# Where six weight buffers and one activation buffer start in SBUF: a layout change in a float32 decoder trunk

## The chip, the cores and the metric

The kernel runs on one core of a Trainium2 chip. The metric is device time in microseconds (us). Engines are named as the profile names them: PE is TensorE (its weight loads are PEld), DVE is VectorE, ACT is ScalarE, POOL is GpSimd, SP is SyncE, which issues most DMAs.

## What is computed

Two decoder layers over 256 tokens of width 1024, all in float32. Layer 0 is a gated linear recurrence with an input projection to 4096 columns and an output projection, then a dense SwiGLU of inner width 2816. Layer 1 is sliding-window attention with a shared key/value projection, then a mixture of 8 experts of inner width 3584, two experts per token.

```python
h = h + hgrn2_mixer(rmsnorm(h), w_in, lb, g_norm, w_out)      # 1024 -> 4096, 1024 -> 1024
h = h + (silu(hn @ w_gate) * (hn @ w_up)) @ w_down             # 1024 -> 2816 -> 1024
k, v = rmsnorm(h) @ kv_w                                       # 1024 -> 512
h = h + swa_attention(rmsnorm(h), k, v, w_q, w_o)              # 1024 -> 1024, twice
h = h + moe_swiglu(rmsnorm(h), router, w_gate, w_up, w_down)   # 8 experts, top 2
```

## The kernel before

The dense stages (everything up to the experts) stream their weights in 63 chunks of 128 partitions x 2048 columns (8 KB a partition). A chunk c lands by DMA in `raw[:, c % 6]`. A product in float32 is made of three matmuls in the reduced format fp32r: ACT copies the chunk, rounded, to `w_hi[:, c % 3]` (line 626), DVE subtracts to get the remainder in `w_lo[:, c % 3]` (line 916), and the activations are split the same way, into `ht_hi` and `ht_lo` for most stages, `mid_hi` and `mid_lo` for the SwiGLU's inner values, `kv_hi` and `kv_lo` for keys and values. `product` (lines 1442 to 1444) then issues hi x hi, hi x lo, lo x hi. Each matmul has two operands in SBUF: the stationary one, 128 columns that a weight load brings into the array, and the moving one, 256 or 512 columns that stream through. The weight load of the next matmul runs beside the moving stream of the present one.

In `to_features` the weights are stationary and the activations move: chunks 0 to 7 and the SwiGLU's 22 gate and up chunks (20 to 41). In `to_rows` the activations are stationary and the weights move: chunks 8 to 15, the outputs 16 to 19 (512 columns wide), the SwiGLU's down chunks 42 to 52 (512 wide), keys 53 and values 58 (256 wide, with `kv_hi`/`kv_lo`), queries 54 to 57 and attention output 59 to 62 (512 wide). In both, the streams that run beside each other come in one order: moving hi beside the load of hi, moving lo beside the load of lo, moving hi beside the load of the next hi.

The expert stage is a loop over expert blocks (8 in this run), each with 46 loads; its matmuls are plain float32 of 32 stationary columns, four of them abreast in the array's column strips, and take their moving operands from a ring made of `raw` and `more_ring` (lines 1888 and 1900). `more_ring` begins where `w_hi` began.

Buffers are laid one behind another, each start rounded up to 32 bytes. In bytes of a partition, `raw` begins at 16512, `h` at 65664, `ht_hi` at 73856, `ht_lo` at 82048, `w_hi` at 114880, `w_lo` at 139456, `mid_hi` at 164032, `mid_lo` at 186560, `kv_hi` at 207040, `kv_lo` at 215232. Modulo 512 bytes that is 128 for `raw`, `h`, `ht_hi` and `ht_lo`, and 192 for all the others. Slots of `w_hi`, `w_lo` and `raw` are 8192 bytes apart, the 128-column pieces that a matmul takes are multiples of 512 bytes apart, so every piece has its buffer's remainder.

Of the kernel before, what the change touches and what calls it, by code (L numbers as in the profile page):

```python
# [9 lines left out]
P = 128  # L10
# [19 lines left out]
CW = 2048  # L30
RAW, SPLIT = 6, 3
# [66 lines left out]
def build_program(nc, a, out):  # L98
    f32, f32r = mybir.dt.float32, mybir.dt.float32r
    i32, u32 = mybir.dt.int32, mybir.dt.uint32  # L100
    ALU, ACT, AX = mybir.AluOpType, mybir.ActivationFunctionType, mybir.AxisListType
    MUL, ADD, SUB = ALU.mult, ALU.add, ALU.subtract

    def plain(ap):
        return ap.bitcast(f32)
# [36 lines left out]
    ctx = ExitStack()  # L142
    with ctx:
        def sb(stack, name, shape, dt=f32):
            return stack.enter_context(nc.sbuf_tensor(name, shape, dt))

        def sem(name):
            return ctx.enter_context(nc.semaphore(name))


        raw = sb(ctx, "raw", [P, RAW, CW])
        h = sb(ctx, "h", [P, TT, D])
        with ExitStack() as over:

            early = sb(over, "early", [P, TT, 2, D])
        ht_hi = sb(ctx, "ht_hi", [P, KT, T], f32r)
        ht_lo = sb(ctx, "ht_lo", [P, KT, T], f32r)
        xs = sb(ctx, "xs", [P, TT, D])
        const = sb(ctx, "const", [P, K_END])
# [24 lines left out]
        early_slot = sb(ctx, "early_slot", [P, TT, 2], u32)  # L184

        dense = ExitStack()
        w_hi = sb(dense, "w_hi", [P, SPLIT, CW], f32r)
        w_lo = sb(dense, "w_lo", [P, SPLIT, CW], f32r)
        s = ExitStack()
        fT = sb(s, "fT", [P, HEADS, T])  # L190
        qT = sb(s, "qT", [P, HEADS, T])
# [49 lines left out]
        slot = sb(ctx, "slot", [P, TT, 2, 4], u32)  # L241
# [39 lines left out]
        hi_ready = sem("hi_ready")  # L281
        split_ready = sem("split_ready")
# [35 lines left out]
        first_hi = sem("first_hi")  # L318
        first_lo = sem("first_lo")
# [73 lines left out]
            return banks[c % 4] if c < 12 else banks[4 + c % 2]  # L393

        def split_view(buf, c, width):
            return buf[:, c % SPLIT, :].rearrange("p (k c) -> p k c", c=width)


        def ring_place(k):
# [211 lines left out]
        def _(act):  # L611
# [9 lines left out]
            def round_chunk(c, slot_raw, raw_count, slot):  # L621
                act.wait_ge(raw_full[slot_raw], raw_count)

                if not (isinstance(c, int) and c < SPLIT):
                    act.wait_ge(chunk_used, c - (SPLIT - 1))
                nc.scalar.activation(w_hi[:, slot, :], raw[:, slot_raw, :], ACT.Copy).then_inc(hi_ready, 1)  # L626

            def round_to(c_last):

                while nxt[0] <= c_last:  # L630
                    c = nxt[0]
                    round_chunk(c, c % RAW, 16 * (c // RAW + 1), c % SPLIT)
                    nxt[0] += 1
# [44 lines left out]
            def round_x(pairs):  # L678
                for u in pairs:
                    act.wait_ge(fresh_turned, u + 1)  # L680
                    for k in range(2):
                        kt = 2 * u + k
                        ins = nc.scalar.activation(ht_hi[:, kt, :], FRESH_1[u][:, T * k:T * k + T], ACT.Copy,
                                                   scale=cols[:, kt:kt + 1])
                    ins.then_inc(fresh_hi, 1)

            half_chunk = lambda buf, part: buf[:, 0, 1024 * part:1024 * part + 1024]
            act.wait_ge(turn_free, 1)
            round_x((0, 1))
            act.wait_ge(first_full, 16)  # L690
            nc.scalar.activation(half_chunk(w_hi, 0), half_chunk(raw, 0), ACT.Copy).then_inc(first_hi, 1)
            round_x((2, 3))
            act.wait_ge(raw_full[0], 16)
            nc.scalar.activation(half_chunk(w_hi, 1), half_chunk(raw, 1), ACT.Copy).then_inc(hi_ready, 1)
            nxt[0] = 1
            round_to(LEAD - 1)
            act.wait_ge(x_loaded[1], 16)
# [7 lines left out]
            for c in range(N_IN):  # L705
# [10 lines left out]
                part, i = divmod(c, 4)  # L716
# [186 lines left out]
        def _(dve):  # L903
# [9 lines left out]
            def rest_chunk(c, slot_raw, slot):  # L913

                dve.wait_ge(hi_ready, c + 1)
                nc.vector.tensor_tensor(w_lo[:, slot, :], raw[:, slot_raw, :], plain(w_hi[:, slot, :]), SUB).then_inc(split_ready, 1)  # L916

            def rest_to(c_last):
                while nxt[0] <= c_last:
                    c = nxt[0]  # L920
                    rest_chunk(c, c % RAW, c % SPLIT)
                    nxt[0] += 1
# [54 lines left out]
            def rest_x(pairs):  # L977
                for u in pairs:
                    dve.wait_ge(fresh_hi, u + 1)
                    for k in range(2):  # L980
                        kt = 2 * u + k
                        ins = nc.vector.scalar_tensor_tensor(
                            out=ht_lo[:, kt, :], in0=FRESH_1[u][:, T * k:T * k + T], scalar=cols[:, kt:kt + 1],
                            in1=plain(ht_hi[:, kt, :]), op0=MUL, op1=SUB)
                    ins.then_inc(fresh_lo, 1)

            half_chunk = lambda buf, part: buf[:, 0, 1024 * part:1024 * part + 1024]
            rest_x((0, 1))
            dve.wait_ge(first_hi, 1)
            nc.vector.tensor_tensor(half_chunk(w_lo, 0), half_chunk(raw, 0), plain(half_chunk(w_hi, 0)), SUB).then_inc(first_lo, 1)  # L990
            rest_x((2, 3))
            dve.wait_ge(hi_ready, 1)
            nc.vector.tensor_tensor(half_chunk(w_lo, 1), half_chunk(raw, 1), plain(half_chunk(w_hi, 1)), SUB).then_inc(split_ready, 1)
            nxt[0] = 1
            rest_to(LEAD - 1)
            turn_copy(cols[:, 16:64], 48)
# [35 lines left out]
            for c in range(N_IN):  # L1032
# [38 lines left out]
                if c == 7:  # L1071
# [6 lines left out]
                    k = 0  # L1078
# [17 lines left out]
                if c in (11, 12, 13):  # L1096
                    j = c - 11
                    k = sum(NCH - 1 - jj for jj in range(j))
# [330 lines left out]
            for t in range(TT):  # L1429
                for half in range(2):  # L1430
                    part = h[:, t, 512 * half:512 * half + 512]
# [4 lines left out]
        def _(pe):  # L1436
# [50 lines left out]
            def to_features(c, bank, hi, lo, fresh=None):  # L1487

                pe.wait_ge(split_ready, c + 1)
                wh, wl = split_view(w_hi, c, 256), split_view(w_lo, c, 256)  # L1490
                for half in range(2):
                    for k in range(KT):
                        if half == 0 and fresh is not None and k in fresh:
                            pe.wait_ge(fresh_lo, fresh[k])
                        cut = slice(P * half, P * half + P)
                        ins = product(bank[:, 256 * half:256 * half + 256], (wh[:, k, cut], wl[:, k, cut]),
                                      (hi[:, k, :], lo[:, k, :]), k == 0, k == KT - 1)
                ins.then_inc(chunk_used, 1)

            def to_rows(c, width, kts, k0, n_k, hi, lo, dst, since=None, tell=False, fresh=None, then_turn=None):  # L1500


                pe.wait_ge(split_ready, c + 1)
                wh, wl = split_view(w_hi, c, width), split_view(w_lo, c, width)
                for t in range(TT):
                    for q in range(max(1, width // 512)):
                        w = min(width, 512)
                        for k in range(kts):
                            kt = k0 + k
                            if t == q == 0:  # L1510
                                split_since(since, kt)
                            if fresh is not None and q == 0 and (t, k) in fresh:
                                pe.wait_ge(fresh_lo, fresh[t, k])
                            tok = slice(P * t, P * t + P)
                            cut = slice(w * q, w * q + w)
                            ins = product(dst(t, q), (hi[:, kt, tok], lo[:, kt, tok]), (wh[:, k, cut], wl[:, k, cut]),
                                          kt == 0, kt == n_k - 1)
                        if k0 + kts == n_k and tell == "parts" and (t, q) != (1, 1):
                            ins.then_inc(part_done, 1)
                        if then_turn is not None and (t, q) == (1, 0):  # L1520
                            turn_fresh(0, 0, then_turn)
                            turn_fresh(0, 1, then_turn)
                    if t == 0 and tell == "tile" and k0 + kts == n_k:
                        ins.then_inc(tile_done, 1)
                ins.then_inc(chunk_used, 1)
                if then_turn is not None:
                    turn_fresh(1, 0, then_turn)
                    turn_fresh(1, 1, then_turn)
# [434 lines left out]
```

## Time and profile before

| | |
|---|---|
| median of 3 runs | 1325.21 us |
| the runs | 1325.21, 1326.4, 1322.11 us |
| span of the profiled execution | 1321.3 us |
| of it, up to the expert loop | 444.1 us |
| of it, the expert loop | 869 us |
| PE busy | 1299.1 us (98%) |
| DVE busy, ACT busy | 360.1 us (27%), 246.4 us (19%) |

The profiled execution's span is 3.9 us (0.3%) under the median of the runs; a run's time may hold a little more than the span from first to last instruction. A matmul's recorded duration (276 ns for 256 columns) is longer than the distance between two matmuls' starts, since they are pipelined. What a matmul costs is that distance, its cadence, and it is read from the start times.

### The profile page before, as it was taken

The numbers are of one execution on the slowest core, as the hardware profiler recorded it, in microseconds if no ns is written. First come the engines' busy times: TensorE is split into PE (matmuls) and PEld (weight loads), VectorE is DVE, ScalarE is ACT, GpSimd is POOL, SyncE is SP. The second block draws the span as 40 slices with busy tenths as digits, with TensorE's granted clock in tenths as the row PEclk, the third lists the DMA queues.
The fourth block names the chain that finished last, engine by engine and source line by source line (L and its number), as shares of the span: only waits on it lengthen the run. The fifth ranks groups of instructions, "written<-read, shape, count | busy, mean of one in ns | idle before, by whom it ended". The sixth has DMA issues, their size and how long they took to land.

```text
span 1321.3 us, 32549 instructions
## 1 busy us (share of the span) xinstructions
PE 1299.1 (98%) x14662; PEld 879.8 (67%) x14662; DVE 360.1 (27%) x539; ACT 246.4 (19%) x370; POOL 56.0 (4%) x50
## 2 busy tenths in 40 slices
PE   8999999999899999999999999999999999999998
PEld 8998899988767533555745655665574575566565
DVE  5875555554875401000000100100100010010011
ACT  5554544443743100000000000000000000000000
POOL 1001000000000320000000000000000000001600
PEclk9999999999999899999999999999999999999999
DMA  9866555565522899999999999999999999999992
GB/s 321 269 210 225 185 182 177 187 223 191 184 96 72 360 421 420 415 419 418 416 419 419 418 418 418 418 410 419 419 404 420 418 407 418 416 409 414 419 413 110
DMA packets 114199, 442.52 MB, mean 335 GB/s; under 512 B 9284, under 2 KB 55700, under 8 KB 83348
## 3 DMA queue, kind: packets, MB, share of 16 engines
q1 hardware_dynamic: 107904, 424.75, 81.5%
q10 hardware_dynamic: 4820, 11.53, 2.5%
q0 software_dynamic: 1344, 4.20, 0.8%
q8 instruction: 120, 1.97, 0.6%
q14 instruction: 11, 0.09, 0.0%
HBM read 434.12 MB, written 12.08 MB: 338 GB/s over the span
## 4 chain that ended last, share of the span: by engine, by line
PE 93%; DVE 3%; ACT 2%; issue 1%; DMA 0%; ACTq 0%; DVEq 0%
PE bank L1888 44%; PE bank L1900 22%; PE bank L1442 8%; PE bank L1444 8%; PE bank L1443 8%; PE bank L1689 1%; PE bank L1600 1%; DVE w_lo L916 1%; ACT w_hi L626 0%; PE bank L1865 0%; DMA const<-in_shape_constants 0%; ACT ht_hi L654 0%; PE bank L1744 0%; PE bank L1940 0%; DVE q_from L1100 0%
## 5 line engine op out<-in xcount | busy, mean ns | idle before, releaser
L1888 PE MATMUL bank<-more_ring,xT 128*32 128x512 f32 (+1 forms) x3456 | 341.0, 545 | 0.0
L1888 PEld LDWEIGHTS bank<-more_ring,xT 128*32 128x32 f32 x3456 | 164.2, 110 | 163.5 <-issue 84.4
L1888 PE MATMUL bank<-raw,xT 128*32 128x384 f32 (+1 forms) x2688 | 259.3, 532 | 0.7 <-DVE xT L1352 0.7
L1888 PEld LDWEIGHTS bank<-raw,xT 128*32 128x32 f32 x2688 | 122.4, 110 | 127.0 <-issue 76.6
L1411 DVE TENSOR_TENSOR e_hid<-e_silu,bank 128x384 f32<-128x384 f32 (+1 forms) x48 | 26.9, 616 | 542.3 <-PE bank L1888 542.3
L1900 PE MATMUL bank<-more_ring,hidT 128*32 128x256 f32 x3072 | 171.4, 379 | 0.0
L916 DVE TENSOR_TENSOR w_lo<-raw,w_hi 128x2048 fp32r<-128x2048 f32 x62 | 141.5, 2289 | 99.1 <-ACT w_hi L626 99.0
L1900 PEld LDWEIGHTS bank<-more_ring,hidT 128*32 128x32 f32 x3072 | 120.8, 110 | 46.4
L1442 PE MATMUL bank<-ht_hi,w_hi 128*128 128x256 f32 x464 | 129.4, 279 | 1.5 <-DVE ht_lo L930 1.5
L1900 PE MATMUL bank<-raw,hidT 128*32 128x256 f32 x2304 | 129.9, 379 | 0.0
L1444 PE MATMUL bank<-ht_hi,w_lo 128*128 128x256 f32 x464 | 128.9, 278 | 0.0
L1443 PE MATMUL bank<-ht_lo,w_hi 128*128 128x256 f32 x464 | 128.9, 278 | 0.0
L626 ACT ACTIVATE w_hi<-raw 128x2048 fp32r<-128x2048 f32 x62 | 118.6, 1918 | 38.7 <-PE bank L1444 38.3
L1900 PEld LDWEIGHTS bank<-raw,hidT 128*32 128x32 f32 x2304 | 91.0, 110 | 37.9 <-issue 0.6
L889 ACT ACTIVATE e_silu<-bank 128x384 f32<-128x384 f32 (+1 forms) x48 | 22.6, 544 | 392.8 <-PE bank L1888 392.8
L1442 PEld LDWEIGHTS bank<-ht_hi,w_hi 128*128 128x128 f32 x464 | 87.9, 189 | 2.5 <-issue 2.4
L1443 PEld LDWEIGHTS bank<-ht_lo,w_hi 128*128 128x128 f32 x464 | 87.9, 189 | 0.0
L1444 PEld LDWEIGHTS bank<-ht_hi,w_lo 128*128 128x128 f32 x464 | 87.9, 189 | 0.0
L892 ACT ACTIVATE yb<-bank 96x512 f32<-96x512 f32 x8 | 4.7, 593 | 441.6 <-PE bank L1900 441.6
L1442 PE MATMUL bank<-w_hi,ht_hi 128*128 128x256 f32 (+1 forms) x224 | 74.4, 332 | 3.7 <-DVE ht_lo L944 1.6
L1444 PE MATMUL bank<-w_hi,ht_lo 128*128 128x256 f32 (+1 forms) x224 | 73.2, 327 | 0.0
L1443 PE MATMUL bank<-w_lo,ht_hi 128*128 128x256 f32 (+1 forms) x224 | 72.9, 326 | 0.0
(284 smaller groups left out, 898.6 us busy)
## 6 DMA issues: line engine op xcount, KB each, us to landing
more_ring<-in_moe_w_up SPq DMA_DIRECT2D x64, 1024.0 KB, 16.2
more_ring<-in_moe_w_down SPq DMA_DIRECT2D x64, 1024.0 KB, 16.9
raw<-in_moe_w_gate SPq DMA_DIRECT2D x64, 768.0 KB, 15.5
more_ring<-in_moe_w_up SPq DMA_DIRECT2D x64, 768.0 KB, 15.8
raw<-in_moe_w_gate SPq DMA_DIRECT2D x48, 1024.0 KB, 16.1
raw<-in_moe_w_down SPq DMA_DIRECT2D x48, 1024.0 KB, 17.5
more_ring<-in_moe_w_gate SPq DMA_DIRECT2D x16, 1024.0 KB
raw<-in_hgrn_w_in SPq DMA_DIRECT2D x15, 1024.0 KB, 11.8
```

The source lines that it names most:

```text
L626: nc.scalar.activation(w_hi[:, slot, :], raw[:, slot_raw, :], ACT.Copy).then_inc(hi_ready, 1)
L889: nc.scalar.activation(e_silu[:, j, 0:w], banks[j][:, 0:w], ACT.Silu).then_inc(e_silu_ready, 1)
L892: nc.scalar.activation(yb[:, 0:512], banks[6][0:CAP, :], ACT.Copy)
L916: nc.vector.tensor_tensor(w_lo[:, slot, :], raw[:, slot_raw, :], plain(w_hi[:, slot, :]), SUB).then_inc(split_ready, 1)
L1411: nc.vector.tensor_tensor(e_hid[:, j, 0:w], e_silu[:, j, 0:w], banks[GRPS + j][:, 0:w], MUL).then_inc(e_hid_ready, 1)
L1442: nc.tensor.matmul(dst, st[0], mv[0], start=first, stop=False)
L1443: nc.tensor.matmul(dst, st[0], mv[1], start=False, stop=False)
L1444: return nc.tensor.matmul(dst, st[1], mv[0], start=False, stop=last)
L1600: whole = lambda bank_rows, at, w, st, mv: nc.tensor.matmul(bank[bank_rows:bank_rows + CH, at:at + w], st, mv, start=True, stop=True)
L1689: nc.tensor.matmul(LOGIT_BANKS[g % 2][b][:, :], const[:, K_ANTI:K_ANTI + P], bias_rev[:, GRP * g:GRP * g + GRP, :][:, heads, 2 * P - P * ( ...
L1888: ins = nc.tensor.matmul(out_banks[j][GTOK * c:GTOK * c + GTOK, 0:w], xT[:, j, kt, :], chunk[:, c], start=kt == 0, stop=kt == KT - 1)
L1900: ins = nc.tensor.matmul(banks[6 + j // 2][GTOK * c:GTOK * c + GTOK, 256 * (j % 2):256 * (j % 2) + 256], hidT[sup][:, g, m, :], ring_place ...
```

## The change

An unused buffer of 64 bytes a partition (16 columns) goes between `ht_hi` and `ht_lo`. The three slots of `w_hi` and the three of `w_lo` become six buffers of their own, `w_split0` to `w_split5`, with unused 64-byte pieces ahead of the second, third, fourth and fifth. All instructions stay as they are, with other addresses.

```diff
         ht_hi = sb(ctx, "ht_hi", [P, KT, T], f32r)
+        sb(ctx, "ht_gap", [P, 16])
         ht_lo = sb(ctx, "ht_lo", [P, KT, T], f32r)
...
-        w_hi = sb(dense, "w_hi", [P, SPLIT, CW], f32r)
-        w_lo = sb(dense, "w_lo", [P, SPLIT, CW], f32r)
+        w_hi, w_lo = [], []
+        for place, (buf, gap) in enumerate(zip([w_hi] * SPLIT + [w_lo] * SPLIT, (0, 16, 16, 16, 16, 0))):
+            if gap:
+                sb(dense, f"w_gap{place}", [P, gap])
+            buf.append(sb(dense, f"w_split{place}", [P, CW], f32r))
...
         def split_view(buf, c, width):
-            return buf[:, c % SPLIT, :].rearrange("p (k c) -> p k c", c=width)
+            return buf[c % SPLIT][:, :].rearrange("p (k c) -> p k c", c=width)
...
-                nc.scalar.activation(w_hi[:, slot, :], raw[:, slot_raw, :], ACT.Copy).then_inc(hi_ready, 1)
+                nc.scalar.activation(w_hi[slot][:, :], raw[:, slot_raw, :], ACT.Copy).then_inc(hi_ready, 1)
...
-                nc.vector.tensor_tensor(w_lo[:, slot, :], raw[:, slot_raw, :], plain(w_hi[:, slot, :]), SUB).then_inc(split_ready, 1)
+                nc.vector.tensor_tensor(w_lo[slot][:, :], raw[:, slot_raw, :], plain(w_hi[slot][:, :]), SUB).then_inc(split_ready, 1)
```

Counting on from `ht_lo` at 82112, the new starts modulo 512 are: `ht_lo` 192; `w_hi` slots 0, 1, 2 at 256, 320, 384; `w_lo` slots 0, 1, 2 at 448, 0, 0; `mid_hi`, `mid_lo`, `kv_hi` and `kv_lo` 0; `more_ring` 256. `ht_hi`, `h` and `raw` stay at 128.

## Rows read from the trace of the kernel before

**Rows 1.** The page: busy time of each engine, and the granted clock in 40 slices.

```profile
PE 1299.1 (98%) x14662; PEld 879.8 (67%) x14662; DVE 360.1 (27%) x539; ACT 246.4 (19%) x370; POOL 56.0 (4%) x50
PEclk9999999999999899999999999999999999999999
```

**Rows 2.** Chain that ended last (start, us, what), and PE's waits (total, times, longest).

```profile
444.11 72.46 PE bank L1888 x768
...
PE bank L1442 <- DVE w_lo L916: 1.3, 1, 1.3
```

**Rows 3.** Stretches: length, busy PE, PEld, DVE, ACT, POOL; clock, DMA share, GB/s.

```profile
11.80:17.30 5.50, 5.50 (x47) 5.50 (x48) 4.68 (x6) 3.98 (x5) 0.94 (x1) 1.00 1.10 348
...
102.80:108.20 5.40, 5.40 (x47) 5.40 (x48) 2.35 (x3) 0.00 (x0) 0.00 (x0) 1.00 0.51 152
...
166.20:264.00 97.80, 97.80 (x866) 97.80 (x865) 54.91 (x46) 41.59 (x34) 0.00 (x0) 1.00 0.57 184
```

**Rows 4.** Instructions in order of time (start, duration), 256-column matmuls with `ht_hi`/`ht_lo`.

```profile
58.32 0.28 PE L1443 MATMUL bank<-w_lo,ht_hi 128*128 128x256 f32 x1
...
58.66 0.28 PE L1443 MATMUL bank<-w_lo,ht_hi 128*128 128x256 f32 x1
...
93.76 0.28 PE L1442 MATMUL bank<-w_hi,ht_hi 128*128 128x256 f32 x1
...
94.47 0.28 PE L1442 MATMUL bank<-w_hi,ht_hi 128*128 128x256 f32 x1
```

**Rows 5.** The same view, 256-column matmuls with `kv_hi`/`kv_lo`.

```profile
333.34 0.28 PE L1444 MATMUL bank<-w_hi,kv_lo 128*128 128x256 f32 x1
...
333.82 0.28 PE L1442 MATMUL bank<-w_hi,kv_hi 128*128 128x256 f32 x1
```

**Rows 6.** The same view, 512-column matmuls: two with `ht_hi`, two with `mid_hi`.

```profile
132.46 0.39 PE L1442 MATMUL bank<-w_hi,ht_hi 128*128 128x512 f32 x1
...
134.29 0.39 PE L1444 MATMUL bank<-w_hi,ht_lo 128*128 128x512 f32 x1
...
271.26 0.39 PE L1442 MATMUL bank<-w_hi,mid_hi 128*128 128x512 f32 x1
...
272.39 0.39 PE L1444 MATMUL bank<-w_hi,mid_lo 128*128 128x512 f32 x1
```

**Rows 7.** The same view, plain float32 matmuls (two records for each instruction).

```profile
101.12 0.39 PE L1620 MATMUL bank<-val,sc 128*128 128x128 f32 x2
101.34 0.39 PE L1621 MATMUL bank<-val,sc 128*128 128x128 f32 x2
...
365.95 2.74 PE L1689 MATMUL bank<-bias_rev,const 128*128 128x512 f32 x6
```

**Rows 8.** Weight loads of line 1442 (count: minimum, median, maximum ns; first and last start).

```profile
L1442 PEld LDWEIGHTS bank<-ht_hi,w_hi x464: 186/188/329, 17.5 to 269.1; 128*128 128x128 f32 x155
...
L1442 PEld LDWEIGHTS bank<-w_hi,kv_hi x32: 190/192/192, 332.6 to 376.3; 128*128 128x128 f32 x32
```

**Rows 9.** Groups of line 1442 by shape (busy us, mean ns); lines 1443, 1444 have as many.

```profile
L1442 PE MATMUL bank<-ht_hi,w_hi 128*128 128x256 f32 x464 | 129.4, 279 | 1.5 <-DVE ht_lo L930 1.5
...
L1442 PE MATMUL bank<-w_hi,ht_hi 128*128 128x512 f32 x96 | 38.7, 404 | 3.7 <-DVE ht_lo L944 1.6 <-DVE w_lo L916 1.3 <-DVE ht_lo L930 0.7
...
L1442 PE MATMUL bank<-w_hi,ht_hi 128*128 128x256 f32 x128 | 35.6, 278 | 0.0
...
L1442 PE MATMUL bank<-w_hi,mid_hi 128*128 128x512 f32 x88 | 34.5, 392 | 0.0
```

**Rows 10.** Groups of the two instructions that split a chunk, on DVE and ACT.

```profile
L916 DVE TENSOR_TENSOR w_lo<-raw,w_hi 128x2048 fp32r<-128x2048 f32 x62 | 141.5, 2289 | 99.1 <-ACT w_hi L626 99.0
...
L626 ACT ACTIVATE w_hi<-raw 128x2048 fp32r<-128x2048 f32 x62 | 118.6, 1918 | 38.7 <-PE bank L1444 38.3
```

**Rows 11.** DMA issues (count, KB each, median us from issue to landing).

```profile
raw<-in_moe_w_gate SPq DMA_DIRECT2D x64, 768.0 KB, 15.5
more_ring<-in_moe_w_up SPq DMA_DIRECT2D x64, 768.0 KB, 15.8
```

More of the change, by code:

```diff
@@ L685, in round_x @@
                     ins.then_inc(fresh_hi, 1)
-            half_chunk = lambda buf, part: buf[:, 0, 1024 * part:1024 * part + 1024]
+            half_chunk = lambda buf, part: buf[:, 1024 * part:1024 * part + 1024]
             act.wait_ge(turn_free, 1)
@@ L690, in _ @@
             act.wait_ge(first_full, 16)
-            nc.scalar.activation(half_chunk(w_hi, 0), half_chunk(raw, 0), ACT.Copy).then_inc(first_hi, 1)
+            nc.scalar.activation(half_chunk(w_hi[0][:, :], 0), half_chunk(raw[:, 0, :], 0), ACT.Copy).then_inc(first_hi, 1)
             round_x((2, 3))
             act.wait_ge(raw_full[0], 16)
-            nc.scalar.activation(half_chunk(w_hi, 1), half_chunk(raw, 1), ACT.Copy).then_inc(hi_ready, 1)
+            nc.scalar.activation(half_chunk(w_hi[0][:, :], 1), half_chunk(raw[:, 0, :], 1), ACT.Copy).then_inc(hi_ready, 1)
             nxt[0] = 1
@@ L985, in rest_x @@
                     ins.then_inc(fresh_lo, 1)
-            half_chunk = lambda buf, part: buf[:, 0, 1024 * part:1024 * part + 1024]
+            half_chunk = lambda buf, part: buf[:, 1024 * part:1024 * part + 1024]
             rest_x((0, 1))
             dve.wait_ge(first_hi, 1)
-            nc.vector.tensor_tensor(half_chunk(w_lo, 0), half_chunk(raw, 0), plain(half_chunk(w_hi, 0)), SUB).then_inc(first_lo, 1)
+            nc.vector.tensor_tensor(half_chunk(w_lo[0][:, :], 0), half_chunk(raw[:, 0, :], 0), plain(half_chunk(w_hi[0][:, :], 0)), SUB).then_inc(first_lo, 1)
             rest_x((2, 3))
             dve.wait_ge(hi_ready, 1)
-            nc.vector.tensor_tensor(half_chunk(w_lo, 1), half_chunk(raw, 1), plain(half_chunk(w_hi, 1)), SUB).then_inc(split_ready, 1)
+            nc.vector.tensor_tensor(half_chunk(w_lo[0][:, :], 1), half_chunk(raw[:, 0, :], 1), plain(half_chunk(w_hi[0][:, :], 1)), SUB).then_inc(split_ready, 1)
             nxt[0] = 1
```

## The prediction, made before the changed kernel was run

> **What bounds the kernel now.** I read the page first: PE is busy for 98% of the span, and its clock is granted in full nearly throughout, 2.4 GHz [rows 1]. So there is hardly a wait to shorten; only the cadence of matmuls can move the time. The chain that ended last says where that cadence counts. It passes over the expert loop in pieces such as 72.46 us for 768 records [rows 2], and that loop is 869 us. Ahead of it lie 444 us, and there the longest wait of a product on a weight remainder is 1.3 us [rows 2]. In the SwiGLU's stretch PE is busy for 97.80 of 97.80 us, while DVE works 54.91 and ACT 41.59 [rows 3].
>
> [...] I cost the shift of `more_ring` from 192 to 256 at nothing on PE. Of the DMAs that fill the ring, a 768 KB load lands in 15.5 us into `raw` and in 15.8 us into `more_ring` [rows 11]: two remainders, no difference that could starve PE. If the new one cost 5% of DMA time PE would wait; nothing here suggests that.
>
> **The dense stages are not at a floor, and there the operands' addresses show.** Three cadences for the same shape of 256 columns, where 256 / 2.4 is 106.7 ns:
> - Usual, with `ht`: three starts in 58.66 - 58.32 = 0.34 us, 113 ns. The long stretch gives the same: 97.80 us for 866 records, less 2.4 that began before it (276 / 113), is 113.3 ns [rows 3, 4]. Moving and stationary buffers are 64 bytes apart modulo 512 (128 against 192).
> - In the first chunk after a break, with the same buffers: six starts in 94.47 - 93.76 = 0.71 us, 118 ns [rows 4]. Four chunks run so, about 189 matmuls; two of them are in the stretches with 47 records in 5.50 and 5.40 us, where 113.3 ns would give 51 and 50 [rows 3].
> - With `kv`, where both operands lie at 192: four starts in 333.82 - 333.34 = 0.48 us, 120 ns [rows 5], and their weight loads take 192 ns where the others take 188 [rows 8].
>
> Whatever ACT and DVE do beside it leaves the 113 alone. [...] At 512 columns: 1.83 us / 8 = 228.8 ns with `ht` (64 bytes apart), 1.13 / 5 = 226 to 227 with `mid` (0 apart), against 213.3 [rows 6]. [...]
>
> **What the change gives each pair.** Call 64 bytes a line and count modulo 8 lines. Before, streams that run together are 1 apart (`ht`) or 0 (`mid`, `kv`). After, hi pairs with `ht` are 2, 3, 4 lines apart for slots 0, 1, 2, lo pairs 4, 3, 3. With `mid` and `kv` the hi pairs are 4, 5, 6 and the lo pairs 7, 0, 0. Hi pairs are two of each three matmuls.
>
> **The sum.** Matmuls [rows 8, 9]: (464 + 16 + 128) x 3 = 1824 of 256 columns with `ht` (16 are line 1562's, of the first chunk); 96 with `kv`; 96 x 3 = 288 of 512 with `ht`; 88 x 3 = 264 with `mid`. No row shows fp32r two lines apart or more, so I bound it. [...] Upper end: 120, the worst row, for 256 columns. I take 111 for 256 columns, the row of the same load beside the same length of stream, and for 512 the middle of 226.7 and 215.5, 221.1, since its row is less like it:
> - 1635 x 2.3 ns = 3.8 us, and 189 x 7 = 1.3 us for the chunks at 118;
> - `kv`: 96 x 2/3 x 9 = 0.6 us (its lo pairs stay at 0);
> - `mid`: 264 x 7/9 x 5.6 = 1.1 us (lo pairs of two slots in three stay at 0);
> - `ht` at 512: 288 x 7.7 = 2.2 us.
>
> Together 9.0 us: the profiled span of 1321.3 would be 1312.3, and the median 1325.2 becomes 1316.
>
> The splits on ACT and DVE change neighbours too. Their means are 1918 and 2289 ns for 2048 columns [rows 10], and PE covers them: it waits 1.3 us in all for a remainder [rows 2]. If that cover were gone, as between stages, some six of each are in the open; 4% of 12 x 2.1 us is 1 us either way. No instruction, wait or DMA is added.
>
> [...]
>
> **Rivals.**
> - *Distance beyond one line is worth nothing.* For: 113 holds with the moving operand a line behind (`to_features`) and a line ahead (`to_rows`), as a floor would; what is left may be the handing over of weights. Then only 118s (0.9 us) and `kv` (0.4 us) gain: 1324. Against: 512 columns show 13 to 15 ns of excess, though the load has ended half way.
>   [...]
> - *Slower: the lines repeat sooner than 512 bytes.* If every 256 bytes, slot 2's hi pairs (4 lines) and slot 0's lo pairs (4) fall together: a third of 1824, 608 x 6.7 ns = +4.1 us, 1329. If every 128 bytes, all of slot 0 and slot 2's hi pairs: 608 x 5/3 x 6.7 = +6.8 us, 1332. For: 0 and 1 are the only distances seen, and ahead and behind cost alike, which a period of two lines would give. It decides if the coinciding pairs cost 120 and the others stay at 113. If instead mixed distances keep PE in the 118 pattern, 1635 x 4.7 = +7.7 us, 1333.
> [...]
>
> **How the numbers follow.** Chances: my forecast, with gains from 5 to 16 us, 0.48; nothing beyond one line 0.29; slower 0.23. A measurement of this kernel tells about 0.3%, 4 us, from no change. The forecast alone spans 1309 to 1321; to leave out no more than 2 in 10 the range runs from 1309 to 1330.
>
> **What would show it.** In the profile after: the stretch of the SwiGLU's gate and up chunks should shrink by 2%, with starts 111 ns apart; 512-column starts should be near 221; `kv` should have two short cadences for each long one; the expert loop should stay 869 us. With the rival, cadences stay 113. With repetition, slots of a chunk differ: two of three at or near 120, one at 113. I am wrong if the expert loop moves, or if the cadences don't depend on the slot or on the distance at all.

## The result, and the profile after

| | before | after |
|---|---|---|
| median (lowest to highest), runs beside each other | 1323.76 us (1322.11 to 1326.4) | 1332.84 us (1331.67 to 1333.83) |
| ratio, 95% interval | | 1.0063 [1.0047, 1.0079] |
| span of the profiled execution | 1321.3 us | 1331.0 us |
| start of the expert loop | 444.11 us | 453.33 us |
| PE busy | 1299.1 us | 1310.7 us |

The changed kernel is slower by about 9 us; the prediction had it faster by 9. The page of the kernel after, answering to [rows 1]: instruction counts as before, the clock granted as before, and PE, which is the bound, busy for 11.6 us more.

```profile
span 1331.0 us, 32549 instructions
...
PE 1310.7 (98%) x14662; PEld 904.9 (68%) x14662; DVE 360.4 (27%) x539; ACT 245.8 (18%) x370; POOL 56.0 (4%) x50
...
PEclk9999999999999899999999999999999999999999
```

The chain that ended last, of after (start, us, what), and one of PE's waits (total, times, longest), answering to [rows 2]:

```profile
453.33 72.81 PE bank L1892 x768
...
1286.16 36.44 PE bank L1904 x669
...
PE bank L1446 <- DVE w_split L920: 1.2, 1, 1.2
```

The loop starts 453.33 - 444.11 = 9.2 us later and ends at 1286.16 + 36.44 = 1322.6, so it still takes 869 us. The loss lies ahead of the loop, and none of it in waits for a weight remainder (1.2 us where it was 1.3). The stretch of the SwiGLU's gate and up chunks, of after, with the columns of [rows 3]:

```profile
166.20:264.00 97.80, 97.80 (x825) 97.80 (x824) 54.33 (x43) 41.89 (x35) 0.00 (x0) 1.00 0.59 186
```

825 matmuls fit in the time of 866. By the prediction's reckoning the cadence is 97.80 / (825 - 2.4) = 118.9 ns, where it was 113.3. Instructions of after in order of time (start, duration). The first six lines are the first and the last hi x hi matmul of one chunk in slot 0, one in slot 1 and one in slot 2, all of 256 columns, with 45 starts from the first to the last; then a stretch of 512 columns with `mid`. Lines 1446 to 1448 are lines 1442 to 1444 of before:

```profile
192.75 0.28 PE L1446 MATMUL bank<-ht_hi,w_split 128*128 128x256 f32 x1
...
198.12 0.28 PE L1446 MATMUL bank<-ht_hi,w_split 128*128 128x256 f32 x1
...
198.47 0.28 PE L1446 MATMUL bank<-ht_hi,w_split 128*128 128x256 f32 x1
...
203.76 0.28 PE L1446 MATMUL bank<-ht_hi,w_split 128*128 128x256 f32 x1
...
204.12 0.28 PE L1446 MATMUL bank<-ht_hi,w_split 128*128 128x256 f32 x1
...
209.51 0.28 PE L1446 MATMUL bank<-ht_hi,w_split 128*128 128x256 f32 x1
...
295.25 0.40 PE L1446 MATMUL bank<-w_split,mid_hi 128*128 128x512 f32 x1
...
296.86 0.39 PE L1447 MATMUL bank<-w_split,mid_hi 128*128 128x512 f32 x1
```

Slot 0: 5.37 us / 45, 119.3 ns. Slot 1: 5.29, 117.6. Slot 2: 5.39, 119.8. `mid`: seven in 1.61, 230, where it was 226 to 227 [rows 6]. A mean over all chunks of one kind (every difference of neighbouring starts in the trace) gives 118.8 ns for stationary weights (113.7 before) and 117.6 where the weights move (114.5 before); 512 columns with `ht` take 231.9 (229.2 before), `mid` 229.6 (226.8 before), `kv` 118.7 in slot 1 and 119.9 in slot 2 (119.9 and 120.0 before).

With those means the cadences alone add up to 1440 matmuls with stationary weights x 5.1 = 7.3 us; 384 with moving weights x 3.1 = 1.2; 288 of 512 columns with `ht` x 2.6 = 0.8; 264 with `mid` x 2.8 = 0.7; `kv` -0.1. Together 9.9 us, against 9.2 in the trace. The start times of each stage show how the 9.2 are made up: the chunks themselves take 8.7 us more (in chunks 0 to 7, waits that became 0.9 us shorter hide a part of the cadence's price), the breaks between stages 1.0 us less, and the first product starts 1.5 us later, at 13.27 us where it was at 11.72. That last part doesn't come from the pairs, for it lies ahead of them: the 16 transposes there, of before and then of after, are

```profile
6.48 1.97 PE L1541 MATMUL bank<-const,h 128*128 128x128 f32 x16
```

```profile
6.95 3.67 PE L1545 MATMUL bank<-const,h 128*128 128x128 f32 x16
```

and e2_slots_by2 below, whose time is that of before, has 3.67 us there as well. In these two executions, then, the operands' addresses account for about 8 of the 9 us.

The groups of the two splits, of after, stand as in [rows 10]; neither engine took more time per instruction:

```profile
L920 DVE TENSOR_TENSOR w_split<-raw,w_split 128x2048 fp32r<-128x2048 f32 x62 | 141.6, 2289 | 105.3 <-ACT w_split L630 105.3
...
L630 ACT ACTIVATE w_split<-raw 128x2048 fp32r<-128x2048 f32 x62 | 118.3, 1912 | 44.8 <-PE bank L1448 44.8
```

### The profile page after: what moved, and what is told of

It reads as the page before. It is cut to its first block, busy times and chain, and to the rows that moved or that the text cites. A ratio compares the mean times of both kernels' runs of the same rounds, so it can differ in the third digit from the quotient of the medians.

```text
span 1331.0 us, 32549 instructions
## 1 busy us (share of the span) xinstructions
PE 1310.7 (98%) x14662; PEld 904.9 (68%) x14662; DVE 360.4 (27%) x539; ACT 245.8 (18%) x370; POOL 56.0 (4%) x50
## 4 chain that ended last, share of the span: by engine, by line
PE 94%; DVE 3%; ACT 2%; issue 1%; DMA 0%; ACTq 0%; DVEq 0%
PE bank L1892 44%; PE bank L1904 22%; PE bank L1446 8%; PE bank L1447 8%; PE bank L1448 8%; PE bank L1693 1%; PE bank L1604 1%; DVE w_split L920 1%; ACT w_split L630 0%; DMA const<-in_shape_constants 0%; ACT ht_hi L658 0%; PE bank L1869 0%; PE bank L1748 0%; PE bank L1944 0%; DVE q_from L1104 0%
## 5 line engine op out<-in xcount | busy, mean ns | idle before, releaser
L1892 PEld LDWEIGHTS bank<-more_ring,xT 128*32 128x32 f32 x3456 | 174.4, 110 | 154.0 <-issue 61.1
L1892 PEld LDWEIGHTS bank<-raw,xT 128*32 128x32 f32 x2688 | 128.2, 110 | 121.2 <-issue 61.1
L920 DVE TENSOR_TENSOR w_split<-raw,w_split 128x2048 fp32r<-128x2048 f32 x62 | 141.6, 2289 | 105.3 <-ACT w_split L630 105.3
L1446 PE MATMUL bank<-ht_hi,w_split 128*128 128x256 f32 x464 | 131.5, 283 | 1.5 <-DVE ht_lo L934 1.5
L1447 PE MATMUL bank<-ht_lo,w_split 128*128 128x256 f32 x464 | 131.7, 284 | 0.0
L1448 PE MATMUL bank<-ht_hi,w_split 128*128 128x256 f32 x464 | 131.1, 282 | 0.0
L630 ACT ACTIVATE w_split<-raw 128x2048 fp32r<-128x2048 f32 x62 | 118.3, 1912 | 44.8 <-PE bank L1448 44.8
L1446 PEld LDWEIGHTS bank<-ht_hi,w_split 128*128 128x128 f32 x464 | 88.4, 191 | 2.4 <-issue 2.4
L1448 PEld LDWEIGHTS bank<-ht_hi,w_split 128*128 128x128 f32 x464 | 88.6, 191 | 0.0
L1447 PEld LDWEIGHTS bank<-ht_lo,w_split 128*128 128x128 f32 x464 | 88.2, 190 | 0.0
L1446 PE MATMUL bank<-w_split,ht_hi 128*128 128x256 f32 (+1 forms) x224 | 74.9, 334 | 3.5 <-DVE ht_lo L948 1.6
L1447 PE MATMUL bank<-w_split,ht_hi 128*128 128x256 f32 (+1 forms) x224 | 73.7, 329 | 0.0
L1448 PE MATMUL bank<-w_split,ht_lo 128*128 128x256 f32 (+1 forms) x224 | 73.6, 329 | 0.0
```

Of the source, the lines that this page charges most:

```text
L630: nc.scalar.activation(w_hi[slot][:, :], raw[:, slot_raw, :], ACT.Copy).then_inc(hi_ready, 1)
L920: nc.vector.tensor_tensor(w_lo[slot][:, :], raw[:, slot_raw, :], plain(w_hi[slot][:, :]), SUB).then_inc(split_ready, 1)
L1446: nc.tensor.matmul(dst, st[0], mv[0], start=first, stop=False)
L1447: nc.tensor.matmul(dst, st[0], mv[1], start=False, stop=False)
L1448: return nc.tensor.matmul(dst, st[1], mv[0], start=False, stop=last)
L1892: ins = nc.tensor.matmul(out_banks[j][GTOK * c:GTOK * c + GTOK, 0:w], xT[:, j, kt, :], chunk[:, c], start=kt == 0, stop=kt == KT - 1)
```

## The experiments

All experiments move buffers by half a line to a few lines of 64 bytes and change no instruction. `hi` and `lo` pairs are what the prediction calls so: `w_hi` with `ht_hi`, `w_lo` with `ht_lo`. D is the distance of such a pair in lines, weights minus activations; before it is 1 for both. Every kernel has the six buffers of their own, so that one list says where they lie: (part, slot, lines left free ahead of it), part 0 being hi and part 1 lo. What this replaces in the changed kernel:

```diff
-        sb(ctx, "ht_gap", [P, 16])
...
-        w_hi, w_lo = [], []
-        for place, (buf, gap) in enumerate(zip([w_hi] * SPLIT + [w_lo] * SPLIT, (0, 16, 16, 16, 16, 0))):
+        w_hi, w_lo = [None] * SPLIT, [None] * SPLIT
+        for place, (part, slot, gap) in enumerate(LAYOUT):
             if gap:
-                sb(dense, f"w_gap{place}", [P, gap])
-            buf.append(sb(dense, f"w_split{place}", [P, CW], f32r))
+                sb(dense, f"w_gap{place}", [P, 16 * gap])
+            (w_lo if part else w_hi)[slot] = sb(dense, f"{('w_hi', 'w_lo')[part]}{slot}", [P, CW], f32r)
```

LAYOUT stands for the list that each diff below shows; a list with no free lines lays the six buffers one behind another, as before. All results first, then each run:

| run | D of hi, of lo | median us | ratio to before [95%] | loop starts, us |
|---|---|---|---|---|
| before | 1, 1 | 1324 | 1 | 444.1 |
| after | by slot: hi 2, 3, 4; lo 4, 5, 5 | 1332.8 | 1.0063 [1.0047, 1.0079] | 453.3 |
| e1_w_up1 | 2, 2 | 1333.3 | 1.0076 [1.0057, 1.0095] | 452.5 |
| e1_ht_lo_up1 | 1, 0 | 1333.7 | 1.0079 [1.0062, 1.0096] | 448.6 |
| e1_slots | 1, 2, 3 by slot | 1331.9 | 1.0066 [1.0049, 1.0084] | 451.4 |
| e1_lo_up1 | 1, 2 | 1332.9 | 1.0073 [1.0056, 1.0091] | 451.1 |
| e2_w_up2 | 3, 3 | 1330.1 | 1.0044 [1.0028, 1.0059] | 449.3 |
| e2_w_up3 | 4, 4 | 1332.4 | 1.0062 [1.0043, 1.0082] | 453.0 |
| e2_slots_by2 | 1, 3, 5 by slot | 1324.1 | 1.0004 [0.9992, 1.0015] | 443.7 |
| e2_w_half | 1.5, 1.5 | 1332.2 | 1.0058 [1.0043, 1.0073] | 451.7 |
| e3_no_ht_gap | by slot: hi 1, 2, 3; lo 4, 5, 5 | 1329.8 | 1.0042 [1.0028, 1.0056] | 448.4 |
| e3_all_up1 | 1, 1 | 1321.2 | 0.9991 [0.998, 1.0002] | 442.1 |
| e3_lo_up2 | 1, 3 | 1324.9 | 1.0009 [0.9993, 1.0025] | 443.5 |
| e3_ht_up1 | 0, 0 | 1333.2 | 1.0074 [1.005, 1.0098] | 452.9 |

(The prediction counts the shorter way round eight lines, so it calls 5 lines 3. Both are odd.)

A loop start is that of one execution, and it moves with the granted clock too. Two stretches, of before and of e3_all_up1, with the columns of [rows 3]:

```profile
147.00:155.00 8.00, 7.87 (x55) 7.90 (x56) 5.60 (x7) 5.73 (x5) 0.90 (x2) 0.79 0.21 62
```

```profile
147.00:155.00 8.00, 8.00 (x71) 8.00 (x71) 6.21 (x7) 5.46 (x6) 0.90 (x2) 1.00 0.27 84
```

A clock of 0.79 is the mean of two parts. In before it was 0.50 up to about 150.8 us and 1.00 behind that; one stretch of the first part, with its clock, and two starts of 256 columns in it, of before:

```profile
147.50:150.70 3.20, 3.20 (x17) 3.20 (x17) 1.54 (x4) 3.20 (x4) 0.90 (x2) 0.50 0.00 0
```

```profile
147.47 0.41 PE L1444 MATMUL bank<-ht_hi,w_lo 128*128 128x256 f32 x1
...
150.67 0.35 PE L1444 MATMUL bank<-ht_hi,w_lo 128*128 128x256 f32 x1
```

Sixteen starts in order, 3.20 us / 15 = 213.3 ns for 256 columns; after, whose chunk 20 has its pairs four and five lines apart, has the same 213.3 at the clock of 0.50. Half of it is 106.7 ns, or 2.4 columns a ns at the full clock. That is what the runs show behind the prediction's 2.4, 106.7 and 213.3: no row gives the clock itself in GHz. Chunk 20, which falls into it, takes 7.0 to 7.2 us in before, after, e1_w_up1, e2_w_up2, e2_w_up3 and e3_ht_up1, and 5.4 to 5.7 in the other eight, whatever their addresses. So a loop start of one of these eight is to be read as some 1.5 us too early beside the 444.1 of before; the cadences below are free of it.

For most runs one row is shown: the same 90 us of each trace, 170 to 260, which hold nothing but the SwiGLU's gate and up chunks (stationary weights); for some also 64 to 84, where the weights move. The columns are those of [rows 3], and the number to read is the first count. A count of n gives a cadence of 90 us / (n - 2.4). The kernel before, then the one after:

```profile
64.00:84.00 20.00, 20.00 (x179) 20.00 (x178) 16.64 (x20) 16.43 (x16) 0.00 (x0) 1.00 0.63 209
170.00:260.00 90.00, 90.00 (x796) 90.00 (x795) 50.84 (x41) 38.13 (x32) 0.00 (x0) 1.00 0.57 181
```

```profile
64.00:84.00 20.00, 20.00 (x172) 20.00 (x172) 15.22 (x19) 13.91 (x16) 0.00 (x0) 1.00 0.63 208
170.00:260.00 90.00, 90.00 (x759) 90.00 (x758) 49.82 (x41) 38.98 (x32) 0.00 (x0) 1.00 0.59 188
```

796 is 113.4 ns, 759 is 118.9.

### e1_w_up1: one distance for all, two lines

```diff
+        for place, (part, slot, gap) in enumerate(((0, 0, 1), (0, 1, 0), (0, 2, 0), (1, 0, 0), (1, 1, 0), (1, 2, 0))):
```

> All six weight buffers one line (64 bytes) up together, nothing between ht_hi and ht_lo: weights and ht are 2 lines apart in every pair instead of 1, with all parts and slots alike. Distance theory (only the distance between the moving operand and the next weights counts, one line is good and more is bad): 256-column starts 117 to 120 ns apart, 444 us of dense stages become 453, time 1333. Sameness theory (PE settles at 113 ns as long as hi and lo parts and all slots have the same remainder, and any mix keeps it at 117 to 120): 113 ns, time 1324 as before.

```profile
170.00:260.00 90.00, 90.00 (x761) 90.00 (x760) 50.17 (x40) 38.80 (x32) 0.00 (x0) 1.00 0.58 187
```

118.7 ns in every chunk with `ht` but one, whether weights are stationary or move, and 232.5 for 512 columns. So slots at different distances are not needed for the loss: one distance of two lines alone is as slow as the whole change.

### e1_ht_lo_up1: only the activations' remainders moved

`sink`, an existing buffer of 64 bytes, is laid between `ht_hi` and `ht_lo` instead of further behind, so the weights stay. Of other buffers only the small and unsplit ones between `ht_lo` and the old place of `sink` move along, by the same line.

```diff
         ht_hi = sb(ctx, "ht_hi", [P, KT, T], f32r)
+        sink = sb(ctx, "sink", [P, QH])
         ht_lo = sb(ctx, "ht_lo", [P, KT, T], f32r)
...
-        sink = sb(ctx, "sink", [P, QH])
...
+        for place, (part, slot, gap) in enumerate(((0, 0, 0), (0, 1, 0), (0, 2, 0), (1, 0, 0), (1, 1, 0), (1, 2, 0))):
```

> Only ht_lo one line up (the 64-byte buffer sink is laid between ht_hi and ht_lo, so the weights stay where they were): hi pairs 1 line apart, lo pairs 0. Distance theory: two of three starts at 113 ns, the lo pair at 120, mean 115.6, so 1824 x 2.3 ns = +4 us, 1328. Sameness theory: hi and lo parts differ, so 117 to 120 throughout the chunks with ht, +7 to +9 us, 1332.

```profile
170.00:260.00 90.00, 90.00 (x766) 90.00 (x766) 51.22 (x41) 37.72 (x33) 0.00 (x0) 1.00 0.59 184
```

117.8 ns in every chunk. In the gate and up chunks that is a mean start difference of 120 where the lo operands meet (D 0) and of 116.7 elsewhere; where the weights move, the 120 stands at another pair. One coinciding pair in three takes all three out of 113.3; the cost isn't a sum over pairs, as the prediction had it. The runs of this kernel lay wider than those of others, 1328.0 to 1335.3 us. The clock goes with it (granted 0.997 and 0.998 in the two fastest, 0.993 and 0.994 in the other three), and the profiled run is the fastest of the five and one of the eight with the full clock in chunk 20, so that its loop start, 4.5 us late, shows less of the loss than its median.

### e1_slots: a distance for each slot, 1, 2 and 3 lines

```diff
+        for place, (part, slot, gap) in enumerate(((0, 0, 0), (1, 0, 0), (0, 1, 1), (1, 1, 0), (0, 2, 1), (1, 2, 0))):
```

> The buffers of slot 0, 1 and 2 at lines 3, 4 and 5 (hi and lo of a slot alike), ht as before: distances 1, 2, 3 by slot. Distance theory: slot 0 at 113 ns, slots 1 and 2 at 117 to 120, two thirds of +9 us, 1330. Sameness theory: within a chunk all parts are alike, so 113 ns in all three slots, 1324; if sameness across slots counts as well, all at 117 to 120, 1333.

```profile
170.00:260.00 90.00, 90.00 (x764) 90.00 (x764) 51.22 (x41) 37.71 (x33) 0.00 (x0) 1.00 0.58 184
```

Slot 1, two lines, is at 118.4 to 118.8 in every chunk. Slots 0 and 2, one and three lines, are at 117.8 in most and at 113.3 to 114.0 in four chunks before 155 us. With `kv` this layout gives a distance of one line, the other way round, in slot 1, where before it was 0; instructions in order of time of e1_slots:

```profile
377.17 0.28 PE L1447 MATMUL bank<-w_hi,kv_lo 128*128 128x256 f32 x1
...
377.51 0.28 PE L1447 MATMUL bank<-w_hi,kv_lo 128*128 128x256 f32 x1
```

Three starts in 0.34 us, 113 ns. The same chunk of before, 58, has a mean of 119.9, and the other `kv` chunk [rows 5] 120: `kv`'s 120 came from the addresses, not from what precedes it.

### e1_lo_up1: only the weights' remainders moved, one line

```diff
+        for place, (part, slot, gap) in enumerate(((0, 0, 0), (0, 1, 0), (0, 2, 0), (1, 0, 1), (1, 1, 0), (1, 2, 0))):
```

> Only the three w_lo buffers one line up: hi pairs 1 line apart, lo pairs 2. Distance theory: two of three starts at 113 ns, one at 117 to 120, mean 115, about +3 to +4 us, 1328. Sameness theory: 117 to 120 in all, 1332.

```profile
170.00:260.00 90.00, 90.00 (x764) 90.00 (x763) 51.22 (x41) 37.72 (x33) 0.00 (x0) 1.00 0.59 185
```

118.2 ns: as with e1_ht_lo_up1, one third of the pairs at a bad distance is enough. After these four runs two theories stood: any departure from one distance of one line is bad ("near is good"), or even distances are bad and odd ones good.

### e2_w_up2: one distance for all, three lines

```diff
+        for place, (part, slot, gap) in enumerate(((0, 0, 2), (0, 1, 0), (0, 2, 0), (1, 0, 0), (1, 1, 0), (1, 2, 0))):
```

> All six weight buffers two lines up together: 3 lines from ht in every pair, an odd number. Parity theory (an odd number of 64-byte lines between the moving operand and the next weights lets PE hold 113.3 ns, an even number never does): the chunks with ht come back to 113.3, time 1324, no change from before; at most 117.8 where the slow of the two odd states is kept. Nearness theory (only exactly one line is good): 117 to 119 throughout, 1332.

```profile
64.00:84.00 20.00, 20.00 (x179) 20.00 (x178) 15.70 (x19) 16.01 (x17) 0.00 (x0) 1.00 0.63 196
170.00:260.00 90.00, 90.00 (x766) 90.00 (x766) 51.20 (x41) 37.73 (x32) 0.00 (x0) 1.00 0.58 185
```

Where the weights move, 179 matmuls in 20 us, exactly as before: 113.3 at three lines. In the gate and up chunks the same distance runs at 117.8 from first to last, the pattern that before had only in four chunks. An odd distance thus has two cadences, and which one holds is not set by the distance.

### e2_w_up3: one distance for all, four lines

```diff
+        for place, (part, slot, gap) in enumerate(((0, 0, 3), (0, 1, 0), (0, 2, 0), (1, 0, 0), (1, 1, 0), (1, 2, 0))):
```

> The same, three lines up: 4 lines from ht, an even number. Both theories: no chunk at 113.3, cadence 118.7 to 120, time 1332 to 1335. It is here to see whether 4 lines equal 2 (118.7) or 0 (120).

```profile
170.00:260.00 90.00, 90.00 (x752) 90.00 (x751) 49.72 (x41) 38.96 (x32) 0.00 (x0) 1.00 0.58 187
```

90 / 749.6 = 120.1 ns: four lines cost what coinciding operands cost [rows 5], and 512 columns with `ht` take 228.2 in the mean, down from 229.2 towards the 226.7 of `mid` at distance 0 [rows 6]. So the 120 of distance 0 is back at 256 bytes.

### e2_slots_by2: a distance for each slot, 1, 3 and 5 lines

```diff
+        for place, (part, slot, gap) in enumerate(((0, 0, 0), (1, 0, 0), (0, 1, 2), (1, 1, 0), (0, 2, 2), (1, 2, 0))):
```

> Slots 0, 1, 2 at lines 3, 5 and 7, hi and lo alike, ht at 2: distances 1, 3, 5, all odd, and all slots different. Parity theory: 113.3 ns in all slots, handed from chunk to chunk, time 1324. Nearness theory: slot 0 at 113 or 118, the others at 117 to 119, 1331. If even odd distances lose the good state whenever the distance changes from one chunk to the next: 117.8 in all, 1331.

```profile
170.00:260.00 90.00, 90.00 (x796) 90.00 (x795) 50.45 (x41) 38.52 (x32) 0.00 (x0) 1.00 0.58 183
```

Every slot at another distance, up to five lines, and the count is that of before. This is the run that decides between the two theories: 113.4 ns with slots at 1, 3 and 5 lines, so neither nearness nor sameness counts, oddness does. The other stretch, 64 to 84, has 174 where before has 179: chunks 10 to 12 run at 117.8 there, so here too the slower of the two cadences turns up in places where before hasn't got it.

### e2_w_half: one and a half lines

Each `16 * gap` is `8 * gap` here, 32 bytes.

```diff
+        for place, (part, slot, gap) in enumerate(((0, 0, 1), (0, 1, 0), (0, 2, 0), (1, 0, 0), (1, 1, 0), (1, 2, 0))):
...
+                sb(dense, f"w_gap{place}", [P, 8 * gap])
```

> All six weight buffers up by half a line, 32 bytes: 1.5 lines from ht. If 64 bytes are the grain and only the line that a start lies in counts, this is as one line: 113.3 ns, 1324. If the distance itself counts, it lies between 113.3 and 118.7, 1324 to 1333.

```profile
64.00:84.00 20.00, 20.00 (x169) 20.00 (x168) 14.57 (x19) 14.49 (x16) 0.00 (x0) 1.00 0.57 195
170.00:260.00 90.00, 90.00 (x761) 90.00 (x760) 51.06 (x41) 37.91 (x31) 0.00 (x0) 1.00 0.58 186
```

118.7 with stationary weights, 120 with moving ones: half a line is no way out. One value doesn't show what other fractions do.

### e3_no_ht_gap: the change without the gap between the activations

```diff
+        for place, (part, slot, gap) in enumerate(((0, 0, 0), (0, 1, 1), (0, 2, 1), (1, 0, 1), (1, 1, 1), (1, 2, 0))):
```

> The change without its 64 bytes between ht_hi and ht_lo: w_hi slots at lines 3, 4, 5, w_lo slots at 6, 7, 7, ht at 2. Distances of hi pairs 1, 2, 3, of lo pairs 4, 5, 5. Parity theory: slot 0 has even lo pairs, slot 1 even hi pairs, slot 2 none; every second or third chunk throws PE out of the 113.3 state, so 117 to 120 everywhere, time 1331 to 1333. If the gap between ht_hi and ht_lo were the cause of the change's loss: 1324 to 1327.

```profile
170.00:260.00 90.00, 90.00 (x776) 90.00 (x775) 51.22 (x41) 37.72 (x33) 0.00 (x0) 1.00 0.56 183
```

In this layout slot 0 has its hi pair odd and its lo pair even, slot 1 the other way round, slot 2 both odd. In order of time, of e3_no_ht_gap, a stretch each of slots 2, 0 and 1:

```profile
183.79 0.28 PE L1445 MATMUL bank<-ht_hi,w_hi 128*128 128x256 f32 x1
...
184.47 0.28 PE L1445 MATMUL bank<-ht_hi,w_hi 128*128 128x256 f32 x1
...
189.23 0.28 PE L1445 MATMUL bank<-ht_hi,w_hi 128*128 128x256 f32 x1
...
189.93 0.28 PE L1445 MATMUL bank<-ht_hi,w_hi 128*128 128x256 f32 x1
...
194.88 0.28 PE L1445 MATMUL bank<-ht_hi,w_hi 128*128 128x256 f32 x1
...
195.59 0.28 PE L1445 MATMUL bank<-ht_hi,w_hi 128*128 128x256 f32 x1
```

Six starts each: 0.68 us (113), 0.70 (117), 0.71 (118). By the medians the weights' places alone give 1329.8 - 1324.2 = 5.6 of the 9.1 us; the gap between the activations, which shifts every hi pair by a line more, makes up the rest. (The loop starts differ by 4.3, but this execution is one of the eight with the full clock in chunk 20.) From chunk 26 on the slot with both pairs odd is fast between two that are not; in earlier chunks it is at 117.7 to 118.9, but for chunk 5. The expectation had 117 to 120 everywhere and 1331 to 1333, so that much of it missed: an odd chunk can come back to 113.3 right after a chunk with an even pair.

### e3_all_up1: everything one line up, all distances kept

```diff
+        sb(ctx, "ht_gap", [P, 16])
         ht_hi = sb(ctx, "ht_hi", [P, KT, T], f32r)
-        sb(ctx, "ht_gap", [P, 16])
...
+        for place, (part, slot, gap) in enumerate(((0, 0, 0), (0, 1, 0), (0, 2, 0), (1, 0, 0), (1, 1, 0), (1, 2, 0))):
```

> 64 unused bytes ahead of ht_hi: everything from ht_hi on moves one line, so ht is at 3 and the weights at 4, every address of the matmuls' operands is new and every distance as before. If the distance is what counts: 113.3 ns, 1324. If absolute places count (their place against raw and h, or the line itself): 117 to 120, 1332.

```profile
170.00:260.00 90.00, 90.00 (x797) 90.00 (x796) 49.88 (x42) 39.05 (x32) 0.00 (x0) 1.00 0.56 184
```

Activations at 192 and weights at 256 modulo 512 run as those at 128 and 192, so in this one shift only the difference counts. The 2 us by which the loop starts earlier are for the most part chunk 20 at the full clock.

### e3_lo_up2: only the weights' remainders moved, two lines

```diff
+        for place, (part, slot, gap) in enumerate(((0, 0, 0), (0, 1, 0), (0, 2, 0), (1, 0, 2), (1, 1, 0), (1, 2, 0))):
```

> Only w_lo two lines up (one line up cost 9 us): hi pairs 1 line apart, lo pairs 3. Parity theory: all odd, so PE can stay at 113.3 though hi and lo parts differ, 1324; if it takes the slower of the two odd states, 117.8 and 1331. Sameness theory, already weak: 117 to 120, 1332.

```profile
64.00:84.00 20.00, 20.00 (x173) 20.00 (x172) 16.18 (x20) 15.97 (x16) 0.00 (x0) 1.00 0.62 200
170.00:260.00 90.00, 90.00 (x795) 89.90 (x794) 50.26 (x41) 38.71 (x32) 0.00 (x0) 1.00 0.55 182
```

The same edit as e1_lo_up1, one line further: 795 in place of 764. Where the weights move it sits at 117.8, the mirror image of e2_w_up2.

### e3_ht_up1: activations one line up, all pairs coincide

```diff
+        sink = sb(ctx, "sink", [P, QH])
         ht_hi = sb(ctx, "ht_hi", [P, KT, T], f32r)
...
-        sink = sb(ctx, "sink", [P, QH])
...
+        for place, (part, slot, gap) in enumerate(((0, 0, 0), (0, 1, 0), (0, 2, 0), (1, 0, 0), (1, 1, 0), (1, 2, 0))):
```

> ht_hi and ht_lo both one line up (sink is laid ahead of them), weights where they were: both at line 3, distance 0 everywhere. Parity theory: 120.0 ns in every chunk with 256 columns, as kv has it, 1824 x 6.7 ns less what was at 118, +11 us, 1335; the 512-column chunks go down from 229 to 227.

```profile
170.00:260.00 90.00, 90.00 (x752) 90.00 (x751) 49.72 (x41) 39.02 (x32) 0.00 (x0) 1.00 0.57 188
```

120.0 ns, the count of e2_w_up3: 0 and 4 lines are the same. There are only two executions of this kernel, 1333.14 and 1333.16 us. This trace also rules out a rival that the prediction put aside in one sentence: that the cadence comes from what ACT and DVE do meanwhile. They work 39.02 and 49.72 of the 90 us, on and off, and every single start difference inside chunks 23 to 41 is 120 ns, with them and without them.

### What the fourteen traces say together

| distance in lines | 256 columns | 512 columns, weights moving |
|---|---|---|
| 0, 4 | 120.0 ns | 226.7 (with `ht` 228 in the mean) |
| 2, 6 | 118.7 | 232 to 233 |
| 1, 3, 5, 7 | 113.3 or 117.8 | 1 and 5: 229; 3 and 7: 233 |
| hi and lo pairs from different rows | 116.7 to 120 | 228.6 to 234.5 |

The cadence of 113.3 stands only in chunks whose pairs are all odd, in every trace; it is not guaranteed there (slot 1 of after has 3 and 5 lines and runs at 117.7; e2_w_up2 has 3 and 3). No layout beat the kernel before by more than the measurement tells: the best, e3_all_up1, is at 0.9991 with an interval that holds 1.

## Why the prediction was wrong

- *PE is the bound, the dense stages are where addresses count, the expert loop stays.* Right: 9.2 of the 9.7 us between the spans lie ahead of the loop, and the loop stays at 869 us [rows 2]. But 1.5 of the 9.2 lie ahead of the first product and have nothing to do with the pairs. That the loop would cost nothing more with `more_ring` at 256 was my estimate, and the 869 us bear it out.
- *The three cadences come from the addresses of PE's two operands.* Right for 120 against 113: e3_ht_up1 brought it to `ht`, e1_slots took it from `kv`. Not for the 118, as the fourth point says. By what mechanism two addresses cost each other time, no run shows. That they do, e3_ht_up1 shows: one existing 64-byte buffer laid ahead of the activations turns 1324 us into 1333.2.
- *The step that failed: no row shows two lines or more, "so I bound it", with 111 as the value.* Of two distances, 0 (120 ns) and 1 (113.3 ns), I made a trend in which further is better, and took the lower end of the range, 111 ns and 215.5, from plain float32, whose 128-column records start 110 to 112 ns apart, and whose six records of 512 columns take 2.74 us [rows 7]; these say nothing of fp32r at a new distance. No run shows fp32r at 111, 215.5 or the 221.1 taken for 512 columns, and so none of the sum's gains of 2.3, 7, 9, 5.6 and 7.7 ns a matmul; the lowest means of a chunk, over all traces, are 113.3 and 226.6. At two lines fp32r takes 118.7, at three 113.3 or 117.8, at four 120.0. The two terms for 256 columns with `ht`, 1635 x 2.3 and 189 x 7, together -5.1 us, came out at +8.5. And no chunk of any run undercut 113.3 in its mean, so the gain priced was not there to be had in any layout tried.
- *189 matmuls at 118, priced at 7 ns to be gained each.* I read the 118 after a break as an excess that a better distance would take away. It is the slower of two cadences that the same addresses have. It could become the rule, and in e2_w_up2 did.
- *Pairs priced one by one.* In the sum, and in the rival of coinciding pairs, a pair that is good stays good whatever its neighbours are. e1_lo_up1 and e1_ht_lo_up1 changed a third of the pairs and moved all to 117.8 or 118.2.
- *`kv` -0.6, `mid` -1.1, `ht` at 512 columns -2.2 us.* Measured -0.1, +0.7, +0.8. For 512 columns 0 lines is the lowest cadence seen (226.7), not the middle of a range down to 215.5.
- *ACT and DVE unaffected.* Right: 1912 and 2289 ns [rows 10].
- *The far end, 16 us and 1309.* It took every pair at 109 and 215.5 ns, an estimate that no run shows: the lowest chunk means are those 113.3 and 226.6, and the fastest kernel, e3_all_up1, is at 1321.2.
- *Rivals.* The slower one had the outcome in its third form, "mixed distances keep PE in the 118 pattern", at 1333 us; measured 1332.8. Its first form had the period right (every 256 bytes: e2_w_up3 has 120.1 ns at four lines), but left two lines at 113, which gave 1329. That 1333 was hit to the microsecond is in part luck: it prices all pairs at 118, where the slots show 119.4, 117.7 and 119.4, and 1.5 us come from ahead of the first product. Having both periods and the 118 pattern in view, I gave all three together less than a quarter, though for 256 columns the only two distances known were, as it turned out, the best and the worst, and [rows 4] showed that an odd distance could run at 118. A chance near a half for the slower case would have fitted what the rows showed.

Still open: what moves PE between 113.3 and 117.8 at an odd distance. Before, it falls into 118 after breaks between stages, not after all; e2_w_up2 and e3_lo_up2 have it in opposite stages, and chunk 0 is at 117.8 in before and at 113.7 in e3_all_up1, which has the same distances. No run here was made to tell what sets it.

## What to carry to other kernels

Where each fp32r matmul of 256 columns loads new weights, keep the moving and the stationary operand an odd multiple of 64 bytes apart (113.3 or 117.8 ns in these runs, against 118.7 at two lines and 120.0 at none or four), in all pairs that take turns; two layouts moved by multiples of 128 bytes cost nothing (e2_slots_by2 at 1.0004, e3_lo_up2 at 1.0009), a third, e2_w_up2, cost 0.4% by falling into the slower cadence, and every one with an even distance in it cost 4 to 7 ns in 113 in nearly all chunks concerned, 0.4 to 0.8% of a kernel that is only a third dense. Half a line was no better than an even distance (118.7 and 120 ns in e2_w_half). Before moving a buffer, take the cadence from start times for each distance the kernel already has, and don't draw a line through two of them: try the next distance, or price it at the worst seen. A cadence that already occurs now and then, with the same addresses, is a state that an edit can make permanent: the 118 of four chunks of before is the 117.8 of all gate and up chunks in e2_w_up2.

## What the runs showed of the hardware

- At the full granted clock, 256 columns of fp32r take 113.3, 117.8, 118.7 or 120.0 ns, each held over some 20 chunks in a row in one run or another. I had not expected two steady cadences for the same instructions at the same addresses.
- 256 and 512 columns don't agree on the best distance: coinciding operands are worst at 256 columns (120.0 against 113.3) and best at 512 (226.7 with `mid`, 227.9 with `ht` in e3_ht_up1, against 229.2 in before).
- The DMAs of the expert ring landed sooner in two kernels. DMA issues of after, answering to [rows 11], then of e3_all_up1:

```profile
raw<-in_moe_w_gate SPq DMA_DIRECT2D x64, 768.0 KB, 9.6
more_ring<-in_moe_w_up SPq DMA_DIRECT2D x64, 768.0 KB, 9.6
```

```profile
raw<-in_moe_w_gate SPq DMA_DIRECT2D x64, 768.0 KB, 10.8
more_ring<-in_moe_w_up SPq DMA_DIRECT2D x64, 768.0 KB, 10.7
```

Those two are the kernels with `more_ring` at 256 modulo 512; in the twelve others it is at 192, and the same loads took 14.2 to 16.2 us. Other buffers are a line up in both as well, so which of them it is was not separated. PE is busy for 820.0 of 820 us in the loop of before (460 to 1280), and the loop's time didn't change: 869 us in before and in both of these.
